# Grouped top-2 experts on one core: the sorting pass of the token rows replaced by a gather inside each job

## What is computed

```python
def grouped_moe(x, w_router, router_bias, w_gate, w_up, w_down):
    scores = jax.nn.sigmoid((x @ w_router).astype(jnp.float32))
    ...
    masked = jnp.where(jnp.repeat(gmask, EXPERTS_PER_GROUP, axis=-1), sel, NEG_INF)
    _, idx = lax.top_k(masked, TOP_K)
    ...
    for e in range(N_EXPERTS):
        h = jax.nn.silu(x @ w_gate[e]) * (x @ w_up[e])
        y = y + combine[..., e:e + 1] * (h @ w_down[e])
    return y
```

## Time and profile before

| | us |
|---|---|
| median of 3 runs | 1483.64 |
| lowest and highest | 1482.21, 1486.89 |
| the profiled execution | 1487.16 |
| its span (first to last instruction) | 1485.3 |
| PE busy | 1243.5 (84%) |
| DVE busy | 430.4 (29%) |
| ACT busy | 147.7 (10%) |
| weights and inputs moved | 559.39 MB |
| granted TensorE clock, mean | 0.947 |

### The profile page before, as it was taken

One profiled execution on the slowest core, in us unless ns is written; L12 is line 12 of the kernel. 1 busy time (PEld: TensorE's weight loads), 2 busy tenths in 40 slices (PEclk: granted clock), 3 DMA queues, 4 the chain that ended last, 5 costly groups with the idle time before them and its releaser, 6 DMA issues.

```text
span 1485.3 us, 18646 instructions
## 1 busy us (share of the span) xinstructions
PE 1243.5 (84%) x7756; PEld 530.1 (36%) x7757; DVE 430.4 (29%) x812; ACT 147.7 (10%) x255; POOL 76.2 (5%) x138
## 2 busy tenths in 40 slices
PE   3899999899999999879969969978768767857855
PEld 2555644455445564323323323222222221221221
DVE  3211696577655351111110210111111111111112
ACT  3000100234200032100000000000000000000000
POOL 0111200011222000000000000000000000000000
PEclk9899999999999999999999989999988989988988
DMA  9999668666789778899999999999999999999996
GB/s 374 419 389 390 274 234 336 234 229 242 255 329 387 288 283 359 340 426 428 424 428 429 428 428 429 426 428 427 429 429 428 428 429 428 428 429 428 428 427 289
DMA packets 56849, 559.39 MB, mean 377 GB/s; under 512 B 6624, under 2 KB 6624, under 8 KB 19680
## 3 DMA queue, kind: packets, MB, share of 16 engines
q1 hardware_dynamic: 41904, 502.48, 81.1%
q0 software_dynamic: 14320, 52.01, 9.4%
q10 hardware_dynamic: 576, 4.19, 0.7%
HBM read 556.57 MB, written 2.10 MB: 376 GB/s over the span
## 4 chain that ended last, share of the span: by engine, by line
PE 47%; DMA 44%; DVE 5%; issue 2%; ACT 1%; DVEq 0%; ACTq 0%; POOL 0%; SPq 0%
DMA ring<-w_gate_dram 11%; DMA ring<-w_up_dram 10%; PE ps L860 8%; PE ps L855 7%; PE ps L578 7%; DMA ring<-w_down_dram 5%; DMA big<-w_up_dram 5%; PE ps L887 4%; DMA ring<-w_half_dram 4%; DMA big<-w_gate_dram 4%; PE ps L681 3%; DMA ring<-w_in_dram 3%; PE ps L572 3%; PE ps L881 2%; PE ps L821 2%; PE ps L583 2%
## 5 line engine op out<-in xcount | busy, mean ns | idle before, releaser
L855 PE MATMUL ps<-ring,early 128*32 128x256 f32 x1888 | 125.3, 407 | 50.0 <-DMA ring<-w_up_dram 22.5
L860 PE MATMUL ps<-ring,early 128*64 128x512 f32 x560 | 138.7, 631 | 22.5 <-DMA ring<-w_gate_dram 11.9
L1566 DVE TENSOR_TENSOR big<-ps,big 128x1024 f32<-128x1024 f32 x60 | 70.7, 1219 | 267.8 <-PE ps L802 142.1
L578 PE MATMUL ps<-ring,big 128*128 128x512 f32 x320 | 146.0, 598 | 0.0
L1190 DVE SCALAR_TENSOR_TENSOR once<-ring,silu_c,once 128x1024 f32<-128x1024 f32 x96 | 123.2, 1283 | 45.5 <-DMA ring<-w_half_dram 38.7
L881 PE MATMUL ps<-ring,once 128*32 128x512 f32 x576 | 87.2, 722 | 45.3 <-DMA ring<-w_down_dram 45.1
L681 PE MATMUL ps<-ring,big 128*128 128x512 f32 x256 | 115.6, 609 | 1.3 <-ACT big L1075 1.3
L855 PEld LDWEIGHTS ps<-ring,early 128*32 128x32 f32 x1888 | 57.9, 115 | 130.4 <-issue 47.0
L578 PEld LDWEIGHTS ps<-ring,big 128*128 128x128 f32 x320 | 59.1, 191 | 69.4 <-issue 69.3
L855 PE MATMUL ps<-big,early 128*32 128x256 f32 x800 | 57.6, 431 | 29.8 <-DMA big<-w_up_dram 20.9
L887 PE MATMUL ps<-ring,once 128*64 128x512 f32 x336 | 77.3, 598 | 2.3 <-DMA ring<-w_down_dram 2.3
(11 more groups left out here) (320 smaller groups left out, 1031.4 us busy)
## 6 DMA issues: line engine op xcount, KB each, us to landing
ring<-w_down_dram SPq DMA_DIRECT2D x48, 2048.0 KB, 25.6
ring<-w_up_dram SPq DMA_DIRECT2D x47, 2048.0 KB, 25.3
ring<-w_gate_dram SPq DMA_DIRECT2D x32, 2048.0 KB, 25.5
ring<-w_half_dram POOLq DMA_DIRECT2D x96, 512.0 KB, 6.4
big<-w_up_dram SPq DMA_DIRECT2D x17, 2048.0 KB, 22.7
ring<-w_mix_dram SPq DMA_DIRECT2D x32, 1024.0 KB, 12.1
big<-w_gate_dram SPq DMA_DIRECT2D x16, 2048.0 KB, 25.5
late<-w_down_dram SPq DMA_DIRECT2D x16, 2048.0 KB, 23.7
```

The source lines that it names most:

```text
L578: mm = pe.matmul(ps[:, b + t, :], nT[:, k, t * P:(t + 1) * P], w, start=(k == 0), stop=(k == KT - 1))
L855: mm = pe.matmul(out_b[0][BASE * f:BASE * (f + 1), :], rows[0][:, k, :], w[:, kk, f * 256:(f + 1) * 256], start=(k == 0), stop=(k == KT - 1))
L860: mm = pe.matmul(out_b[1][REST * f:REST * (f + 1), :], rows[1][:, k, :], w[:, kk, f * N:(f + 1) * N], start=(k == 0), stop=(k == KT - 1))
L1566: tt(y, Yb[:, 2 * h:2 * h + 2, :].rearrange("p a n -> p (a n)"), y, ALU.add).then_inc(summed, 1)
```

## The change

The sorting pass is gone, with its one-hot matrix, its order numbers and its buffer `xg_all`. Instead every job gathers the rows of the job behind it: DVE builds a one-hot matrix of 96 slots from the table's column j+1 right behind the hidden product, PE gathers in four pieces of four blocks, after the second, third, fourth and fifth down chunk, into the banks `Yb`, and ACT saves them to `xg` with norm and modulation. For that the residual rows have to stay as they are until the end, so ACT copies them in job 0 to a buffer `total` (the place of pair slot 6, once job 0 has used it), and the output sums are added up there. Place 7 in `big` becomes a seventh pair slot for all jobs; which pair goes where is a list, `next_pairs`, and `last_use` gives the chunk that each pair waits for. Job 0 takes its pairs from the slots in another order, and its pairs 0 and 1 are in the ring slots 0 and 1.

```diff
+        total = nT_all[:, 0:TT * D].rearrange("p (t d) -> p t d", t=TT)
+        first_pairs = (0, 1, 8, 2, 3, 6, 7, 4, 5, 0, 1, 2)
+        next_pairs = (3, 4, 7, 0, 1, 2, 3, 4, 5, 0, 1, 2)
...
+        def last_use(p):
+
+            s = next_pairs[p]
+            if s in next_pairs[:p]:
+                return 2 * max(q for q in range(p) if next_pairs[q] == s) + 1
+            return 2 * max(q for q in range(JPAIR) if s in (first_pairs[q], next_pairs[q])) + 1 - JCH
...
-            for i, s in enumerate(first_pairs):
+            for i in (5, 2, 0, 1, 3, 4, 6, 7, 8, 9, 10, 11):
+                s = first_pairs[i]
...
                 else:
-                    sp.wait_ge(slot_free, used_job(2 * (i - 7) + 1))
+                    sp.wait_ge(slot_free, used_job(2 * first_pairs.index(s) + 1))
...
                 for i in range(JPAIR):
-                    sp.wait_ge(slot_free, j * JCH + used_job(2 * i + 1 - JOB_SLOTS))
+                    sp.wait_ge(slot_free, j * JCH + used_job(last_use(i)))
...
-            def sort_rows(blocks):
-                pe.wait_ge(oh_ready, 1)
-                for k in blocks:
-                    if k > 1:
-                        pe.wait_ge(sorted_saved, k - 1)
+            def gather_next(j, i):
+
+                if i == 0:
+                    pe.wait_ge(oh_ready, j + 1)
+                if i % 2 == 0:
+                    pe.wait_ge(summed, j * 4 + (3 + i // 2))
+                for k in range(4 * i, 4 * i + 4):
+                    at = k % 4 * BLK
                     for t in range(TT):
-                        mm = pe.matmul(S[k % 2], tokens[:, t, k * P:(k + 1) * P], oh_all[:, t, :],
+                        mm = pe.matmul(Yb[:, i, at:at + BLK], tokens[:, t, k * P:(k + 1) * P], oh_rows[:, t, :],
                                        start=(t == 0), stop=(t == TT - 1))
-                    mm.then_inc(sort_done, 1)
+                mm.then_inc(next_gathered, 1)
...
-                if first:
-                    sort_rows(range(0, KT // 2))
-                else:
+                if not first:
                     scatter(j, 1, parts=ahead)
...
                     mm.then_inc(slot_free, 1)
+                    if 1 <= i <= 4:
+                        gather_next(j, i - 1)
...
                 if first:
-                    save_sorted(range(0, KT // 2))
+                    act.wait_ge(slot_free, used_job(2 * first_pairs.index(6) + 1))
+                    for t in range(TT):
+                        last = copy(total[:, t, :], tokens[:, t, :])
+                    last.then_inc(total_ready, 1)
...
+                for k in range(KT):
+                    if k % 4 == 0:
+                        act.wait_ge(next_gathered, j * 4 + (k // 4 + 1))
+                    at = k % 4 * BLK
+                    last = act.activation(xg[:, k, :], Yb[:, k // 4, at:at + BLK], ACT.Identity,
+                                          bias=modcol[:, 3, k, 0:1], scale=scale_ffn[:, k:k + 1])
+                last.then_inc(xg_ready, 1)
...
                 last.then_inc(hidden_ready, 1)
+                for t in range(TT):
+                    last = ts(oh_rows[:, t, :], k_("slots"), job[:, 0, t, bass.ds(j + 1, 1)], rs_tok[:, t:t + 1],
+                              ALU.is_equal, ALU.mult)
+                last.then_inc(oh_ready, 1)
...
-                    y = tokens[:, t, h * 1024:(h + 1) * 1024]
+                    y = total[:, t, h * 1024:(h + 1) * 1024]
```

More of the change, by code:

```diff
@@ L141, in constants @@
         "mask1": np.where(c >= p, 0, -BIG),
-        "slots": one * np.arange(2 * SEQ)[None],
+        "slots": one * np.arange(BLK)[None],
         "slots_n": one * (np.arange(P) % BASE)[None],
@@ L375, in used_job, with loads @@
             return used_chunk(NPRE + i)
+        def loads(s, j, p):
+            each = next_pairs.count(s)
+            return j * each + (first_pairs.count(s) - each + next_pairs[:p + 1].count(s))
+        def last_use(p):
[3 more added lines that the diff above has]
+            return 2 * max(q for q in range(JPAIR) if s in (first_pairs[q], next_pairs[q])) + 1 - JCH
         dve_count = [0]
@@ L726, in _ @@
                         for t in range(TT):
-                            mm = pe.matmul(T[0:CAND, 128:129], cand[:, t, 0, :], ones[:, 0:1],
+                            pe.matmul(T[0:CAND, 128:129], cand[:, t, 0, :], ones[:, 0:1],
+                                      start=(t == 0), stop=(t == TT - 1))
+                        for t in range(TT):
+                            mm = pe.matmul(T[0:1, 130:131], cand[:, t, 0, FIRST_EXPERT:FIRST_EXPERT + 1], ones[:, 0:1],
                                            start=(t == 0), stop=(t == TT - 1))
[L729 to L733, removed]
+                        mm.then_inc(pos_done, 1)
                     elif part == 2:
@@ L876, in experts @@
                 for i in range(8):
-                    if i == 4 and first:
-                        sort_rows(range(KT // 2, KT))
                     w = arrived(16 + i)
@@ L896, in any_job @@
                     few, some = (pe.value_load(n_i[0:1, bass.ds(j + i * JOBS, 1)], min_val=0, max_val=1)
[L897 removed]
+                                 for i in (1, 2))
                 with pe.If(few):
@@ L930, in _ @@
             few = pe.value_load(n_i[0:1, bass.ds(jobs + (JOBS - 1), 1)], min_val=0, max_val=1)
+            pe.wait_ge(xg_ready, jobs)
             with pe.If(few):
@@ L1100, in _, with job_evac @@
             act.wait_ge(table_ready, 1)
-            jobs = act.value_load(n_i[0:1, 4 * JOBS:4 * JOBS + 1], min_val=2, max_val=JOBS - 1)
-            def job_rows(at):
-                span = big[:, bass.ds(at + SORTED, KT * 2 * SEQ)].rearrange("p (k s) -> p k s", k=KT)
-                return copy(xg, span[:, :, 0:BLK]).then_inc(xg_ready, 1)
-            def save_sorted(blocks):
-                for k in blocks:
-                    act.wait_ge(sort_done, k + 1)
-                    act.activation(xg_all[:, k, :], S[k % 2], ACT.Identity, bias=modcol[:, 3, k, 0:1],
-                                   scale=scale_ffn[:, k:k + 1]).then_inc(sorted_saved, 1)
-            def job_evac(j, parts, at, first):
+            jobs = act.value_load(n_i[0:1, NUMBERS:NUMBERS + 1], min_val=2, max_val=JOBS - 1)
+            def job_evac(j, parts, first):
                 act.wait_ge(slot_free, j * JCH + used_job(7))
@@ L1455, in _ @@
             last.then_inc(mask_ready, 1)
-            for i, n in ((2, 16), (4, 17)):
-                last = tt(rt[:, n], k_("e16").unsqueeze(1).broadcast_to([P, TT, NE]),
-                          small[:, i:i + 2].unsqueeze(2).broadcast_to([P, TT, NE]), ALU.is_gt)
-            link(last)
-            link(tt(rt[:, 16], rt[:, 16], rt[:, 17], ALU.add))
-            tt(rt[:, 18, 0, :], rt[:, 16, 0, :], rt[:, 16, 1, :], ALU.add).then_inc(shift_ready, 1)
             first = rt[:, 15, :, FIRST_EXPERT]
```

123 lines of the change are left out of this document (46 added, 77 removed).

## The result

The changed kernel takes 1496.37 us (median of five runs, 1491.12 to 1500.62), the kernel before 1483.64 (1482.21 to 1486.89). The ratio is 1.0072, 95% interval 1.0044 to 1.0099, or 6.5 to 14.7 us more. In a later call (run f0_after, the same kernel once more) it was 1.0048 (1.0030 to 1.0067), 1493.34 us. So it is slower, by 0.3% at the least, as forecast. For that second measurement 0.5 to 1.0% had been expected and 124 to 126 us from the start of job 2 to that of job 4, from 4 to 6 and from 6 to 8: the ratio came out just under that, and the three times were 124.5, 124.9 and 124.5 us.

The account below looks back on a forecast made before the run. The prediction took DMA transfers to bound the kernel after 611 us, PE work costing only where the queue empties. A 14.3 us gain and 21.9 us loss gave +7.6 us, from 1483.64 to 1491.2 us, range 1482 to 1498.

Parts of the forecast that it names:

- What bounds the kernel: After 611 us the end is a count of bytes; PE work costs only where it empties the DMA queue.
- The head: Job 0 and job 1's first pairs: earlier issues remove empty queue, a gain of 14.3 us, kept as 12.5 to 16.
- The gather: Every job: 64 records after down chunks 1 to 4 add 7.8 us of PE, 8.0 with DVE's share.
- The jobs of one part are free: Jobs of one part: PE waits for data there, so 7.8 us more fit into these waits at no cost.
- The loss in jobs 2, 4 and 6: Jobs of both parts: PE falls further behind, the next job's pairs go out late; 8.0 + 6.3 + 7.6 = 21.9 us.
- clock rival: Jobs 2, 6 and tail: gather fills waits, clock stays 2.4 GHz, saving 3.2 and 1.7 us; 1485 us, chance 0.18.
- The extra slot doesn't help there: Ends of jobs 2, 4, 6: only two waits are relaxed; pairs where the queue runs dry still wait for chunks 19, 21, 23.
- The tail stays: End of the kernel: scatter and output only read another buffer, so no change in time.
- The sum: Whole kernel: -14.3 + 21.9 = +7.6 us, taking the median from 1483.64 to 1491.2 us.
- that the pair jobs lose little: Rival, jobs of both parts: the gather is hidden, below 2 us a job; time 1471 us, chance 0.10.
- a smaller gain in the head: Rival, jobs 0 and 1: holdups beyond 5 us of slack take half of the gain; 1498 us, chance 0.10.
- Dearer restarts: Rival, next job's fourth and fifth pairs also find the queue dry: 1.4 us more a job; 1497 to 1501, chance 0.12.

Follow-up runs that it names:

- e3: Changed kernel with the gather in jobs of one part (job 0 excepted) cut to one matmul a piece instead of eight: 1492.49 us, ratio 1.0055.
- e4: Changed kernel with the gather cut to one matmul a piece only in jobs 2, 4 and 6: 1479.91 us, ratio 0.9965.
- e1: Changed kernel with only the list of pair slots altered, so pairs 3 to 6 wait for chunks 17, 19, 21, 23: 1479.28 us, ratio 0.9965.
- f4: Changed kernel with the four gather pieces after down chunks 4 to 7 instead of 1 to 4, counted from 0: 1512.21 us, ratio 1.0169.
- f1: Changed kernel with another list of pair slots and PE's last wait for gathered rows moved into the branch's two arms: 1479.28 us, ratio 0.9951.
- e2: Changed kernel with the list of pair slots set back to the six of before, place 7 serving job 0 alone: 1495.23 us, ratio 1.0078.
- f3: Changed kernel with job 0's pairs in the order and slots of before: 1498.41 us, ratio 1.0084.

## Why the prediction was right, step by step

**What bounds the kernel: right.** "A piece of PE work costs nothing unless it leaves the DMA queue empty": e3 and e4 are this sentence in numbers, nothing that can be told for the gather in twelve jobs, and 13 us for it in three.

**The head, -14.3 us: right, -13.7 measured.** Of the 14.3 us 0.35 lie before job 0, so 13.95 is what the 13.7 answers to. The three down pairs go out from 550.93, 2.0 us after job 0's start; counted were the 1.93 us of chunks 0 and 1. From 556 us on the queue is never empty: DMA share 1.01 in 556:586. One thing was not in the working: PE stands 4.47 us at the start of job 1, in "issue", against 1.99 before; and that was hidden, as 556:586 and 586:633 run at 428 and 427 GB/s without a gap. ACT's two copies ran from 561.36 to 565.05, counted from job 0's start 0.7 us ahead of their place in the working.

**The gather, 7.8 us of PE a job: right to the tenth.** Job 4 of before and job 2 of after both run at full clock: PE is busy 72.39 us and 80.20, 7.81 more. A piece is 2.02 us in the timeline alone and 1.95 by difference. The Trainium skill ("TensorE: Matmul & The Clock Gate", LDWEIGHTS) gives a 128-column load 107 ns; 7.81 us over 64 records is 122 ns, so the row was the better guide and by that figure the job would have been 1 us too short.

**The jobs of one part are free: right** (e3). A step of two jobs shows how near the end of that room is: PE is 118.2 us busy of 124.6, while the transfers need 117.4. In e1, at a clock of 1.00, the same 1024 records are 116.6 us busy. So even with unlimited depth a step could hardly go under 117 to 118 us, an estimate from these three numbers, and e1's 119.5 to 121.3 is close to it.

**The loss in jobs 2, 4 and 6, +21.9 us: mechanism right, size 2.2 us too large.** The steps of 124.6 us, the jobs of 81.3, the dips and the pairs issued to an empty queue are all as told. The term that was mis-sized is the lateness of jobs 2 and 6: "8.0 us more PE" holds only at the same clock. Rows 10 show job 2 of before starting at the lower clock, rows 4 show jobs 2 and 6 1.6 us longer than job 4, and after the change all three run at 1.00. With the measured lengths of both, the working gives 81.3 - 74.96 = 6.3 for job 2, 81.3 - 73.44 - 1.7 = 6.2 for job 4, 81.3 - 75.08 - 0.4 = 5.8 for job 6: 18.3. Measured are 7.2, 7.1 and 5.5.

That is the prediction's clock rival (chance 0.18), and its part in the three jobs came true beside the forecast, not in its place. The argument against it, that the wait before a job's first pair stays 3 us, did not hold in the changed kernel: it is 1.2 to 1.95 us there. That the added work raises the clock is shown by e3, which takes most of it away, by the clock of the whole (0.9615 for 0.970 and 0.967). How it acts at one start is not shown. Over the profiled executions of all kernels but f4, jobs 2, 4 and 6 began at the full clock in all 16 cases in which PE had waited 1.0 to 1.95 us ahead of them, and at the lower one in 9 of 11 in which it had waited 2.2 to 3.0. But the wait is itself set by the clock a little earlier. The last up pair of the job before and job 2's start in f1, and the last up pair before job 4 in the changed kernel:

```profile
610.89 1.93 PE L861 MATMUL ps<-big,early 128*32 128x256 f32 x32 [2.96 <-DMA big<-w_up_dram]
635.81 1.50 PE L861 MATMUL ps<-ring,early 128*32 128x256 f32 x16 [2.97 <-DMA ring<-w_gate_dram]
```

```profile
732.87 3.30 PE L861 MATMUL ps<-big,early 128*32 128x256 f32 x32 [2.93 <-DMA big<-w_up_dram]
```

From the up pair to the end of the job PE has no wait for data in either, with the same gather. Where the up pair ran at full clock PE is done early and waits 2.97 us; where it ran at the lower one PE is late and waits 1.95 (job 4 at 757.81 above). So it is in all 17 starts, of the changed kernel, e1, e2, e4, f0, f1 and f3, in which PE had waited for that up pair: 11 low ones, then waits of 1.0 to 1.95 us, and 6 at full clock, then 2.8 to 2.97. The changed kernel had six short waits of six in its two profiles, f3, with the same gather, two long ones of three. So the 16 cases don't show the gather at work by themselves, and a full clock at the start of these jobs is not a thing that the change brings for certain. The Trainium skill (same page, "HAM oscillation — how this bites in real kernels") names waits for transfers between bursts of matmuls as what takes the clock down, and advises loops that leave no such waits; e3 against the change agrees, by 0.9615 against 0.970. The rival and the forecast weren't exclusive, and giving them separate times was a fault of the working.

**The extra slot doesn't help there: right** (e2), and it was not made to. The prediction listed the chunks that the pairs wait for, and said that the ones at which the queue runs dry are not relaxed. It didn't go on to the question that this list asks, which table would relax them. That is e1, and it turns a loss of 0.5 to 0.7% into a gain of 0.35 to 0.5%.

**The tail stays: wrong by 1.3 us.** "Scatter and output only read another buffer." From the first scatter record to the end of the span it takes 11.0 us for 9.6 before, and the output's transfers landed later. The groups of the last issues, in the changed kernel and in the kernel before: last the us to landing.

```profile
out_dram<-big SPq DMA_DIRECT2D x3, 512.0 KB, 3.9
```

```profile
out_dram<-big SPq DMA_DIRECT2D x3, 512.0 KB, 2.8
```

The part in front of it did not grow. The gap between PE's last down matmul and the scatter went from 1.4 to 2.6 us, but the last pair's records took 2.2 us (they ran at full clock), not 3.62 (rows 10), and from the landing of the last pair to the first scatter record it is 5.0 us before (1470.67 to 1475.68), 4.9 in the changed kernel (1473.40 to 1478.27), 5.3 in e2 and 5.2 in e3, however long PE's records take in between. So something else may set that time; moving the wait (f1) did not change it. It also means that the clock rival's 1.7 us of tail did not come back: the records were faster and the end was no earlier. Why the same 512 KB land 1.1 us later stays open. All variants show 3.6 to 3.9 us but e3, which has 2.8 like the kernel before; no run was made for it.

**The sum: near, partly by errors that cancel.** +7.6 was predicted, +8.5 measured from job 0's start in the profiled executions, and 6.8 and 12.7 us between the medians of the two calls. Counted from job 0's start the working says +7.95. With the three jobs at the full clock it would have said 3.2 less, +4.7. What it left out made up for that: 0.25 us less in the head, 1.0 in the steps (19.7 against 21.9 - 3.2), 1.2 between job 8 and the last landing, where 425 GB/s stand for 427 and no step of the change was counted, and 1.3 in the tail: +8.5. So the nearness of the two totals is in part luck. The sign doesn't hang on this: it comes from 19.7 us against 13.7, both foreseen within 2.2. The rest of the distance from 1491.2 to 1496.37 is in no step; the start of job 0 moves by up to 10 us between executions, and single traces don't show whether the change has a part in that.

The other rivals: that the pair jobs lose little is refuted by steps of 124.6, and a smaller gain in the head by 84.3 us. Dearer restarts would have given steps of 126 to 127 at the clock of before; three equal steps of 124.6 don't show them, though the measured 7.2 and 7.1 against 6.3 and 6.2 leave room for 0.9 us of them in two of three.

## What to carry to other kernels

Where transfers set the end, price a piece of engine work by the place where the queue is shallowest: here 64 records a job cost nothing that could be told in twelve jobs and 6.6 us each in three. Before adding work to such a place, write down which piece of work frees the slot for each transfer; if an extra buffer doesn't free the ones that run dry earlier, give it to others (e1's table, 14 us). And don't put work that the next stage needs behind the last piece of this one: f4's four pieces, moved by three chunks, cost another 19 us.

## What the runs showed of the hardware

- More work on PE made it faster in part: the granted clock of the whole went from 0.950 to 0.970 with 1024 records more, and back to 0.9615 when those of the one-part jobs were cut to four short ones a job. The place counts too: with the same 1024 records moved behind the last chunks (f4) it was 0.962. Longer waits right ahead of a job mostly came with a low start (f1: 2.97 us), but not always: e1's job 2 starts at full clock after 2.91 us. And a short wait can itself be the trace of a low clock just before it: an up pair of 3.30 us was followed by 1.95 us of wait ahead of the next job, one of 1.93 us by 2.97.
- PE stands 4.47 us at the start of job 1 in the changed kernel (before: 1.99), on nothing that the profile shows as a releaser; the instruction queue moved 0.61 MB before and 0.98 MB now. That the longer code is the cause is argued, not shown. It costs nothing while the DMA queue is full.
- A pair issued into an empty queue lands after 7.5 to 8.6 us, while in a queue that is never empty one pair lands every 4.89 us. What a restart costs over the empty time itself, about 3 us by these two numbers, is an estimate; no run separates the two.
